# Five products a weight block instead of six: low and high parts of 248 tokens side by side in one product

## What is computed

```python
def swiglu(x, wi, wo):
    g, u = jnp.split(x @ wi, 2, axis=-1)
    return (jax.nn.silu(g) * u) @ wo
...
x += 1/2 * post(SwiGLU_1(pre(x)))
x += post(Mixer_i(pre(x)))
x += 1/2 * post(SwiGLU_2(pre(x)))
x += (p[i] @ W_pe) * sigmoid(rmsnorm(x) @ W_pg)
```

## Time and profile before

| | |
|---|---|
| median of 3 runs | 2090.8 us (2090.1 to 2092.8) |
| profiled execution, first to last instruction | 2089.9 us |
| TensorE products | 2068.6 us busy (99%), 17092 instructions |
| TensorE weight loads | 2046.3 us (98%) |
| VectorE | 1125.9 us (54%), 1509 instructions |
| ScalarE | 702.9 us (35%) |
| GpSimd | 47.7 us (2%) |
| chain that ended last | TensorE 86%, VectorE 11%, ScalarE 2% |
| read from memory | 193.78 MB, 95 GB/s over the span |

### The profile page before, as it was taken

How to read it: one execution, slowest core, us unless ns; L and a number is a source line. 1 busy time by engine, 2 the same in 40 slices (tenths; PEclk the granted TensorE clock), 3 DMA queues, 4 the chain that set the end, 5 groups by cost and what they waited for, 6 DMA issues and landing times.

```text
span 2089.9 us, 37944 instructions
## 1 busy us (share of the span) xinstructions
PE 2068.6 (99%) x17092; PEld 2046.3 (98%) x17092; DVE 1125.9 (54%) x1509; ACT 702.9 (34%) x877; POOL 47.7 (2%) x95
## 2 busy tenths in 40 slices
PE   8999999999999999999999999999999999999999
PEld 8999999999999999999999999999998999999998
DVE  6443244866768543244686342344898854323467
ACT  5221123423354322122444222122487432212243
POOL 0000000022200000000000000000000000000000
PEclk9999999999999999999999999999999999999999
DMA  5222222145321322222222222222222222222222
GB/s 175 90 90 89 96 102 81 62 153 162 127 108 61 122 81 92 91 102 92 101 82 101 82 96 89 99 84 79 86 97 84 82 101 102 89 94 85 98 92 82
DMA packets 35106, 202.79 MB, mean 97 GB/s; under 512 B 5088, under 2 KB 5376, under 8 KB 17024
## 3 DMA queue, kind: packets, MB, share of 16 engines
q1 hardware_dynamic: 29520, 183.87, 25.0%
q0 software_dynamic: 5424, 16.50, 2.5%
HBM read 193.78 MB, written 4.48 MB: 95 GB/s over the span
## 4 chain that ended last, share of the span: by engine, by line
PE 86%; DVE 11%; ACT 2%; issue 1%; DMA 1%; DVEq 0%; ACTq 0%
PE acc L1825 70%; PE acc L1935 10%; DVE w_lo L1120 2%; DVE t L1233 2%; PE acc L1866 1%; DVE x L1240 1%; DVE act_lo L1246 1%; DMA raw<-in_weights 1%; DVE rs_post L1228 1%; PE acc L2015 1%; PE acc L2069 1%; DVE xsum L1255 1%; DVE rs_pre L1228 0%; PE acc L2093 0%; PE acc L2142 0%
## 5 line engine op out<-in xcount | busy, mean ns | idle before, releaser
L1825 PE MATMUL acc<-act_hi,w_hi 128*128 128x260 f32 x3072 | 621.5, 284 | 0.0
L1825 PE MATMUL acc<-act_hi,w_lo 128*128 128x260 f32 x3072 | 617.8, 283 | 0.0
L1825 PE MATMUL acc<-act_lo,w_hi 128*128 128x260 f32 x3072 | 617.4, 282 | 0.0
L1825 PEld LDWEIGHTS acc<-act_hi,w_hi 128*128 128x128 f32 x3072 | 472.4, 188 | 2.7 <-issue 2.0
L1825 PEld LDWEIGHTS acc<-act_hi,w_lo 128*128 128x128 f32 x3072 | 472.6, 188 | 0.4
L1825 PEld LDWEIGHTS acc<-act_lo,w_hi 128*128 128x128 f32 x3072 | 471.8, 188 | 0.5
L723 ACT ACTIVATE w_hi<-raw 128x2048 fp32r<-128x2048 f32 (+3 forms) x179 | 323.0, 1805 | 297.4 <-DMA raw<-in_weights 297.3
L1120 DVE TENSOR_TENSOR w_lo<-raw,w_hi 128x2048 fp32r<-128x2048 f32 (+3 forms) x179 | 386.4, 2158 | 31.7 <-ACT w_hi L723 31.7
L1370 DVE TENSOR_TENSOR gu<-acc,rs_pre 128x520 f32<-128x520 f32 x164 | 114.3, 698 | 441.1 <-PE acc L1825 441.0
L849 ACT ACTIVATE hid_hi<-gu 128x520 fp32r<-128x520 f32 x86 | 55.0, 639 | 476.6 <-DVE gu L1390 476.6
L1825 PE MATMUL acc<-hid_hi,w_hi 128*128 128x260 f32 x1024 | 206.4, 283 | 0.2
(11 more groups left out here) (308 smaller groups left out, 2141.6 us busy)
## 6 DMA issues: line engine op xcount, KB each, us to landing
raw<-in_weights SPq DMA_DIRECT2D x138, 1024.0 KB, 4.8
raw<-in_weights SPq DMA_DIRECT2D x32, 896.0 KB, 4.5
ring<-in_k_pages POOLq DMA_DIRECT2D x16, 256.0 KB, 3.7
raw<-in_weights SPq DMA_DIRECT2D x12, 256.0 KB, 5.3
x<-in_x SPq DMA_DIRECT2D x8, 260.0 KB, 6.5
out_y<-x SPq DMA_DIRECT2D x8, 260.0 KB, 2.1
ckb<-ch_rows POOLq DMA_DIRECT2D x8, 256.0 KB, 4.5
ring<-in_v_pages POOLq DMA_DIRECT2D x8, 256.0 KB, 3.8
```

The source lines that it names most:

```text
L1825: ins = nc.tensor.matmul(a[0:width, half, 0:HALF], w[slot][:, at:at + width], m[:, half * HALF:(half + 1) * HALF], start=first and n == 0, ...
```

## The change

The tokens are cut at 248 instead of 260: half 0 has 248 columns, half 1 has 272. High and low parts lie in one tensor, `act[P, 2, KC, TOK]` with the low part first (the same for `hid`, `p_split` and `xc`), so that one operand can take both parts of the first 248 tokens. In a whole tile that isn't in `PLAIN`, a weight block takes five products (`wide_chunk`): high weights times 496 columns, low and high parts of half 0 side by side into bank 0; high weights times the high and times the low part of half 1 (272 each) into bank 1; low weights times the high part of half 0 (248) and of half 1 (272). Half 0 of the result is then two sums, in columns 0 to 247 and 264 to 511 of bank 0, and VectorE adds them when it drains the tile: `scaled` becomes three instructions (a reduction over pairs and two products), `copy_joined` two, `add_joined` three. In `PLAIN` are the first tiles of a feed-forward that are made by `k_outer`, `g1` of sub-layer 0, tile `f`, the `pe` tiles and all tiles of the recurrent mixer. These, the gates and the half pairs keep three products a half, of 248 and 272 columns. A plain tile lies in columns 264 to 783 across both banks, so that it is drained as one piece of 520. In `mixer_out` the order of the products in `halves` changes with it.

```diff
-HALF = TOK // 2
+CUT = 248
+TOKENS = (slice(0, CUT), slice(CUT, TOK))
+WIDTH = (CUT, TOK - CUT)
+WIDE = 2 * max(WIDTH)
+BANK = 512
...
+PLAIN = {f"{s}.{tile}0" for s in range(0, SUBS, 4) for tile in "gu"} | {"0.g1", f"{S_AB}.f"} | \
+        {f"{s}.pe{m}" for s in range(3, SUBS, 4) for m in range(KC)} | {f"{S_C}.{kind}{m}" for kind, m in C_TILES}
...
-        act_hi = sb("act_hi", [P, KC, TOK], F32R)
-        act_lo = sb("act_lo", [P, KC, TOK], F32R)
+        act = sb("act", [P, 2, KC, TOK], F32R)
+        act_lo, act_hi = act[:, 0, :, :], act[:, 1, :, :]
...
+        def whole(a, parts=P):
+
+            return a[0:parts, :, :].rearrange("p a n -> p (a n)")[:, BANK - CUT:BANK - CUT + TOK]
+
+        def out_half(a, half, parts=P):
+
+            return a[0:parts, 0, BANK - CUT:BANK] if half == 0 else a[0:parts, 1, 0:TOK - CUT]
+
+        def out_parts(a):
+
+            return a[:, :, :].rearrange("p a n -> p (a n)")[:, 0:2 * (BANK - CUT)]                .rearrange("p (r n) -> p r n", r=2)[:, :, 0:CUT]
+
+        def added_parts(a):
+
+            return out_parts(a).rearrange("p r n -> p n r")
...
+            def copy_joined(out, name):
+
+                a = acc_of(name)
+                chained(nc.vector.tensor_copy(cols(out, 1), out_half(a, 1)))
+                drains(nc.vector.tensor_reduce(cols(out, 0), added_parts(a), AXX, ALU.add), name)
+
+            def add_joined(out, name):
+
+                a = acc_of(name)
+                ordered(nc.vector.tensor_tensor(cols(out, 0), out_half(a, 0), cols(out, 0), ALU.add))
+                chained(nc.vector.tensor_tensor(cols(out, 1), out_half(a, 1), cols(out, 1), ALU.add))
+                drains(nc.vector.tensor_tensor(cols(out, 0), a[:, 0, 0:CUT], cols(out, 0), ALU.add), name)
...
-                drains(nc.vector.tensor_tensor(two(out), tile_of(J[name]), two(rs_pre[:, :]), ALU.mult), name)
+                if name in PLAIN:
+                    drains(nc.vector.tensor_tensor(out, tile_of(J[name]), rs_pre[:, :], ALU.mult), name)
+                    return
+                a = acc_of(name)
+                ordered(nc.vector.tensor_reduce(cols(out, 0), added_parts(a), AXX, ALU.add))
+                chained(nc.vector.tensor_tensor(cols(out, 1), out_half(a, 1), cols(rs_pre, 1), ALU.mult))
+                drains(nc.vector.tensor_tensor(cols(out, 0), cols(out, 0), cols(rs_pre, 0), ALU.mult), name)
...
-            def chunk(a, slot, at, hi, lo, first, last, width=P):
-
-                for n, (w, m) in enumerate(((w_hi, hi), (w_hi, lo), (w_lo, hi))):
+            def chunk(a, slot, at, split, first, last, width=P):
+
+                hi, lo = split[:, 1, :], split[:, 0, :]
+                for n, (w, part) in enumerate(((w_hi, hi), (w_hi, lo), (w_lo, hi))):
                     for half in range(2):
-                        ins = nc.tensor.matmul(a[0:width, half, 0:HALF], w[slot][:, at:at + width],
-                                               m[:, half * HALF:(half + 1) * HALF],
+                        ins = nc.tensor.matmul(out_half(a, half, width), w[slot][:, at:at + width], cols(part, half),
                                                start=first and n == 0, stop=last and n == 2)
                 return ins
 
-            def parts(hi, lo):
-
-                return lambda c: (hi[:, c, :], lo[:, c, :])
-
-            act_in = parts(act_hi, act_lo)
+            def wide_chunk(a, slot, at, split, first, last):
+
+                hi, lo = split[:, 1, :], split[:, 0, :]
+                high, low = w_hi[slot][:, at:at + P], w_lo[slot][:, at:at + P]
+                nc.tensor.matmul(out_parts(a), high, half_of(split, 0), start=first, stop=False)
+                nc.tensor.matmul(out_half(a, 1), high, cols(hi, 1), start=first, stop=False)
+                nc.tensor.matmul(out_half(a, 1), high, cols(lo, 1), start=False, stop=False)
+                nc.tensor.matmul(out_half(a, 0), low, cols(hi, 0), start=False, stop=last)
+                return nc.tensor.matmul(out_half(a, 1), low, cols(hi, 1), start=False, stop=last)
...
+                    if name in PLAIN:
+                        ins = chunk(a, n % SLOTS, at(c), inp(c), c == 0, c == ks - 1, width)
+                    else:
+                        ins = wide_chunk(a, n % SLOTS, at(c), inp(c), c == 0, c == ks - 1)
...
+                def halves(i):
+
+                    split = inp(chunks[i])
+                    hi, lo = split[:, 1, :], split[:, 0, :]
+                    pe.wait_ge(mixh_ready, n0 + i + 1)
                     for m in range(2):
...
+                        nc.tensor.matmul(out_half(accs[m], 1), weight(w_hi, n, i, m), cols(hi, 1),
+                                         start=i == 0, stop=False)
+                    for m in range(2):
+                        nc.tensor.matmul(out_half(accs[m], 1), weight(w_lo, n, i, m), cols(hi, 1),
+                                         start=False, stop=False)
+                    pe.wait_ge(mixl_ready, n0 + i + 1)
+                    for m in range(2):
+                        nc.tensor.matmul(out_half(accs[m], 1), weight(w_hi, n, i, m), cols(lo, 1),
+                                         start=False, stop=i == KC - 1)
+                        nc.tensor.matmul(out_parts(accs[m]), weight(w_hi, n, i, m), half_of(split, 0),
+                                         start=i == 0, stop=False)
+                        ins = nc.tensor.matmul(out_half(accs[m], 0), weight(w_lo, n, i, m), cols(hi, 0),
+                                               start=False, stop=i == KC - 1)
```

More of the change, by code:

```diff
@@ L2038, in mixer_out @@
-                    product(i, w_lo, hi, False, False)
-                    if kind == "halves":
-                        pe.wait_ge(mixl_ready, n0 + i + 1)
-                    product(i, w_hi, lo, False, i == KC - 1)
+                        halves(i)
+                    else:
+                        third(i)
                 last_pairs(s, inp, 1)
```

191 lines of the change are left out of this document (108 added, 83 removed).

## The result

The change makes the kernel slower, by 0.8%, with an interval that leaves out 1. All times are medians, in device microseconds.

A forecast was written before the change was run, and what follows sets the result against it. TensorE, busy 99% of the span, was taken as the bound by its sum of products. Terms -22.9 + 3.4 + 1.9 + 2.9 + 1.2 + 0.9 = -12.6 us gave a 2078.2 us median, range 2060 to 2097.

The forecast's parts named there:

- What is counted: Weight blocks: 1560 columns stay, one product of six goes; 1448 + 512 + 32 = 1992 wide chunks.
- What a product less is worth: Wide chunks on TensorE: each saves the whole 11.5 ns surplus of a product, -22.9 us over 1992.
- rival A: Every wide tile: surplus goes with columns, a merged product saves 2.6 ns; 5.2 gain, 10.3 stalls, 2095.9 us; 28% with variants.
- Rival B: Wide chunks: 260 columns do not hide the weight load, merging saves 18.8 ns a chunk; 2067.0 us; 15%, stronger form 6%.
- rival C: Wide products: 496 columns run as two pieces (2101 us, 4%), or narrower ones at float32 pace (over 600 us more, 2%).
- Products of half a token set: Half pairs, means and plain tiles: half 0 0.24 us shorter per pair of tiles, half 1 as much longer; zero, within 1 us.
- VectorE's drains: Wide tiles: a drain grows from 0.70 to 1.48 us, mostly hidden by TensorE's work, except at the listed places.
- `hid_lo`: End of each feed-forward: `out0` waits for the last hidden tile's low part, 0.86 x 4 = +3.4 us.
- Samples' keys: Score products waiting for `qbd` behind the drains of `k2` and `k3`: +1.9 us.
- Heads: Attention scores claiming the last tile's accumulator, and the last transposes: +2.9 us (0.8 to 4.4); heads 0 to 2 covered.
- `w_lo` behind a first-half pair: After `out23.0`, the pair covering `w_lo` is 0.24 us shorter: 5 x 0.24 = +1.2 us.
- The mixers' output: `halves` puts four products, not eight, ahead of the low-part wait: 0.3 + 0.4, and 0.2 in attention, +0.9 us.

The follow-up runs named there:

- e1: Kernel before with thirteen streams of 48 products of various widths and types appended behind its last sub-layer; executed once, 496 columns took 224.2 ns, 260 took 119.4.
- e4: Changed kernel with the 496-column product issued as its two 248-column pieces, six products a weight block; 2116.6 us, ratio 1.0125 to the kernel before.
- e9: Kernel before, halves of 260 kept, only feed-forward g and u tiles 3 to 20 and part tiles wide, cut at 248; 2087.4 us, ratio 0.9983.
- e10: Kernel before, halves of 260 kept, only feed-forward g and u tiles 3 to 20 and part tiles wide, cut at 256; 2084.9 us, ratio 0.9971.
- e2: Changed kernel with every tile plain, leaving the cut at 248: six products a weight block, one-operation drains; 2100.0 us, ratio 1.0048 to the kernel before.
- e5: Changed kernel with every tile plain and the cut at 272, so halves of 272 and 248; 2097.2 us, ratio 1.0031 to the kernel before.
- e6: Changed kernel with every tile plain and the cut at 256, so halves of 256 and 264; 2095.9 us, ratio 1.0030 to the kernel before.
- e3: Kernel before, halves of 260 and six products, with VectorE drains as long as the changed kernel's; 2107.3 us, ratio 1.0075.

## Why the prediction was wrong, point by point

**What bounds the kernel: right.** TensorE stayed at 98% of the span, and all that was lost lies in its products, in front of them or in its clock.

**What is counted: right.** 1448 (in the list above), 512 and 32 products of 496 columns, as counted from the earlier trace rows; the count fell by 1992.

**What a product less is worth: wrong, and this is the step that turned the sign.** The surplus of 11.5 ns is there, but it was put down to the product, whatever its width. The streams of e1 split it: 4 ns with the product, 7 with its columns. In place, the merged product gave 3.3 ns (e4 over a feed-forward; 3.8 in its `g` and `u` tiles, 1.7 in its part tiles) or, beside halves of 260, 1.1 (e9) to 3.1 (e10). So -22.9 us should have been -2 to -7. The reason given was a choice of neighbour: the 8-column weights, nearest in type, kept 8.4 of the 11.5 ns, and I read "not the load" as "the product". It only said "not the load", and the 3.1 ns that it gave the load are not in e1's 8-column streams. In the text itself the alternative stood two sentences later, that the surplus may go with columns read at full pace, with 2.6 ns from the float32 rows. That was the right reading, as rival A, at 28%.

**Rival A** asks for 713 ns or more a chunk; 717.5 was measured, and its price of 2.6 ns is the right size. Its time, 2095.9, is nevertheless 11 us too low, because it has the same 10.3 us for the stalls and nothing for the cut. The forecast's own line for being wrong, chunks over 716 ns, is passed. Rival B and rival C are out: a 248-column product takes 114.0 ns and not 119.8 (e1), the two-piece product takes 223.3 ns, no more than the plain one.

**Products of half a token set, "zero, within 1 us": wrong, +9.4 us (e2).** Three things were missed. A begin loses some 0.84 us. My reading is that its second and third stretch wait on work for the second half, now 272 columns, and e5, with the halves the other way round, bears that out for these two stretches; for the first stretch it stays open. Plain chunks at any cut but 260 cost 2 to 4 ns more (e2, e5, e6). And `w_lo` has new waits, 1.7 us in e2. I balanced columns against each other, and did not ask where the shorter ones stand in the order of work.

**VectorE's drains: the size of a drain was right, the places mostly, the sum too low.**
- A wide drain: 1.48 us worked out, 1.48 measured (its four terms as written add to 1.47).
- `hid_lo`: +0.86 forecast, 0.24 to 1.03 measured, +0.79, four times.
- Samples' keys: +1.9 forecast, 1.67 measured.
- Heads: +2.9 forecast with an upper end of 4.4, +4.2 measured. Heads 0 to 2, said to be covered by two tiles, were not: the loads wait 0.24 us at 496.48 and at 515.65, and 0.50 at 535.98.
- `w_lo` behind a first-half pair: +1.2 forecast for five places; 0.80 and 0.17 in each feed-forward, 0.97 x 4, and more at the mixers. The longer drain that stands ahead of `w_lo` on VectorE was left out: with equal halves (e3) TensorE's waits for `w_lo` are 1.7 us, with plain drains (e2) 1.7, with both 3.6.
- The mixers' output: in the attention 0.2 forecast, 0.25 + 0.80 measured. In the recurrent mixer 0.7 forecast; TensorE's wait for high parts there is 2.7 us where it was 4.1, the loads wait 0.5 for low parts, and the whole stretch is 0.04 us longer, a fall of the clock included.
- The clock: the prediction named a fall as a sign of being wrong and gave it no term. The drains alone cost 16.8 us by the medians and 12.1 in e3's execution with the highest clock, against 8.2 for the terms that e3 has (10.3 with `w_lo` and the mixers' output). So waits that were sized too low are 4 us of it, and the clock most of the rest.

**The range, 2060 to 2097,** was too narrow on its upper side because the cut was priced at zero from both sides: no row of before shows a product of 248 or 272 columns or a begin with unequal halves, and such a term wants a bound that is not zero. **Open** remain why equal halves of 260 have the cheapest plain chunks, why 512 + 264 beats 496 + 272 by 2 ns, and which executions have the fall of the clock.

## What to carry to other kernels

A surplus over the ideal pace belongs to the product or to its columns, and one width can't say which: look for the same type at a second width, and where the profile has none, take the smaller share as the likely one. When a change moves a boundary that other stages share, price that boundary in every stage, and try first to keep it local: here the wide product lost 16.5 us with a cut through the whole kernel and gained 3.5 where the same cut was kept to tiles with slack, 6.0 with the cut at 256 there. And where two kernels differ by a few us, put the granted clock of their executions beside the times before naming a cause. A longer drain is paid at each place where the next wait is already near nought, and the list of present waits finds most of these places but not all.

## What the runs showed of the hardware

- fp32r products stream at 4.0 ns + 0.444 ns a column (248 to 496 columns, clock 1.00), bf16 ones at about 2.5 ns + 0.417. 128 columns take 110.6 ns in fp32r. With 8-column weights 260 columns take 122.5 ns in such a stream. (All of e1, one execution.)
- A moving operand and an output in two strided pieces cost nothing more: 223.3 against 224.2 ns at 496 columns.
- A chunk of the same 1560 columns takes 716.3 (e10) to 722.3 ns (e5) in the part tiles, by where it is cut and into how many products.
- The granted clock fell to 0.59 and 0.50 over 460 to 470 us behind two waits of 0.6 and 0.7 us in one execution (e3), and stayed at 1.00 behind waits as long in another (the changed kernel).
- The same kernel took 2102.6 us at a mean granted clock of 0.999 and 2110.3 at 0.995 (e3).
